# DeltaNet heads of a decoder layer: decay rows asked for earlier and used later, roots a step sooner, the output's finish behind the first terms of the inverse

## The reference

```
qkv = silu(causal_depthwise_conv([b_q, b_k, b_v], conv_w))
q, k = l2_normalize(q), l2_normalize(k)
beta = sigmoid(b_beta);  g = -exp(a_log) * softplus(b_dec + dt_bias)
# per chunk, gcum = cumulated g
decay = exp(gcum_i - gcum_j) on and below the diagonal
A = strict_lower(beta_i * (k k^T) * decay)
u, w = solve(I + A, [v*beta, k*beta*exp(gcum)])
v_new = u - w S;  o = (q*exp(gcum)) S + (tril(q k^T) * decay) v_new
S = exp(g_last) S + (k*exp(g_last - gcum))^T v_new
y_B = rms_norm(o, dn_norm_g) * silu(b_z)
```

## Time and profile before

| what | value |
|---|---|
| median of 3 runs | 1997.52 us (1994.28 to 1998.63) |
| the profiled execution | 1999.72 us, its span 1997.9 us |
| TensorE busy | 1941.1 us, 97% of the span |
| VectorE busy | 940.7 us, 47% |
| ScalarE busy | 760.3 us, 38% |
| GpSimd busy | 81.6 us, 4% |
| mean granted clock of TensorE | 0.99 |
| chain that ended last | TensorE 91% |

### The profile page before, as it was taken

How to read it: one execution, slowest core, us unless ns; L and a number is a source line. 1 busy time by engine, 2 the same in 40 slices (tenths; PEclk the granted TensorE clock), 3 DMA queues, 4 the chain that set the end, 5 groups by cost and what they waited for, 6 DMA issues and landing times.

```text
span 1997.9 us, 25728 instructions
## 1 busy us (share of the span) xinstructions
PE 1941.1 (97%) x9812; PEld 1574.3 (79%) x9812; DVE 940.7 (47%) x1266; ACT 760.3 (38%) x1166; POOL 81.6 (4%) x63
## 2 busy tenths in 40 slices
PE   8999999999989989999999999999999999999996
PEld 6886776777868878888787888788888888888885
DVE  6715565576425353531545663774433223323446
ACT  6335455554342433533343334543223113112331
POOL 0000000001202112020000000000000000000000
PEclk9999999999989999999999999999999999999998
DMA  5232212313121221121534444443321111111144
GB/s 187 99 107 81 78 63 94 126 42 137 64 95 64 85 95 57 71 103 46 211 116 154 141 138 143 163 132 101 95 63 43 52 52 42 52 49 45 51 150 148
DMA packets 62031, 191.51 MB, mean 96 GB/s; under 512 B 6720, under 2 KB 6784, under 8 KB 61952
## 3 DMA queue, kind: packets, MB, share of 16 engines
q1 hardware_dynamic: 58496, 184.13, 27.5%
q10 hardware_dynamic: 3456, 6.29, 0.8%
HBM read 146.33 MB, written 44.07 MB: 95 GB/s over the span
## 4 chain that ended last, share of the span: by engine, by line
PE 91%; DVE 4%; DMA 2%; ACT 2%; issue 2%; ACTq 0%; SPq 0%; DVEq 0%
PE gemm L337 18%; PE gemm L339 17%; PE gemm L338 17%; PE gemm L578 5%; PE gemm L579 5%; PE gemm L580 5%; PE dn L1308 2%; PE dn L1306 2%; PE z L1205 2%; PE gemm L1393 2%; PE dn L1227 2%; PE gemm L1394 2%; PE gemm L1395 2%; PE dn L1304 1%; PE dn L1269 1%
## 5 line engine op out<-in xcount | busy, mean ns | idle before, releaser
L337 PE MATMUL gemm<-act_hi,w_hi 128*128 128x512 f32 x1216 | 508.1, 418 | 0.5 <-issue 0.5
L339 PE MATMUL gemm<-act_hi,w_lo 128*128 128x512 f32 x1216 | 476.9, 392 | 0.0
L338 PE MATMUL gemm<-act_lo,w_hi 128*128 128x512 f32 x1216 | 476.4, 392 | 0.0
L329 DVE TENSOR_TENSOR w_lo<-w_raw,w_hi 128x1024 fp32r<-128x1024 f32 x174 | 215.6, 1239 | 240.6 <-ACT w_hi L324 237.1
L324 ACT ACTIVATE w_hi<-w_raw 128x1024 fp32r<-128x1024 f32 x174 | 183.2, 1053 | 278.2 <-PE gemm L339 153.2
L337 PEld LDWEIGHTS gemm<-act_hi,w_hi 128*128 128x128 f32 x1216 | 230.2, 189 | 56.0 <-issue 18.6
L339 PEld LDWEIGHTS gemm<-act_hi,w_lo 128*128 128x128 f32 x1216 | 229.4, 189 | 49.8
L338 PEld LDWEIGHTS gemm<-act_lo,w_hi 128*128 128x128 f32 x1216 | 230.4, 189 | 41.0 <-issue 3.6
L383 ACT ACTIVATE stage<-gemm,cols 128x512 f32<-128x512 f32 x104 | 71.6, 688 | 239.7 <-PE gemm L339 236.0
L1079 ACT ACTIVATE f_t<-f_t 128x512 f32<-128x512 f32 x64 | 40.4, 632 | 218.0 <-DVE f_t L1909 218.0
L1576 DVE TENSOR_TENSOR_SCAN a_P<-a_keep,a_P,a_floor 128x512 f32<-128x512 f32 (+3 forms) x96 | 93.7, 1006 | 26.1 <-ACT a_keep L869 25.9
(11 more groups left out here) (272 smaller groups left out, 2886.0 us busy)
## 6 DMA issues: line engine op xcount, KB each, us to landing
w_raw<-w_stream SPq DMA_DIRECT2D x174, 512.0 KB, 3.7
projections<-stage SPq DMA_DIRECT2D x60, 512.0 KB, 2.9
gate<-projections SPq DMA_DIRECT2D x48, 256.0 KB, 2.7
d_in<-projections SPq DMA_DIRECT2D x12, 512.0 KB, 5.5
x_sb<-xT SPq DMA_DIRECT2D x8, 512.0 KB, 9.0
x_fin<-xT SPq DMA_DIRECT2D x8, 512.0 KB, 4.4
residual<-mixed ACTq DMA_DIRECT2D x16, 256.0 KB, 2.0
act_hi<-residual SPq DMA_DIRECT2D x8, 512.0 KB, 4.8
```

Source lines behind the costliest of these rows:

```text
L329: nc.vector.tensor_tensor(lo[s][:], raw[s][:].rearrange("p (k c) -> p k c", k=KT), hi[s][:].bitcast(f32), ALU.subtract).then_inc(lo_ready[ ...
L337: nc.tensor.matmul(g_bank[hf][:], w_hi[s][:, k, :], a_hi[:, k, t], start=(k == 0), stop=False)
L338: nc.tensor.matmul(g_bank[hf][:], w_hi[s][:, k, :], a_lo[:, k, t], start=False, stop=False)
L339: last = nc.tensor.matmul(g_bank[hf][:], w_lo[s][:, k, :], a_hi[:, k, t], start=False, stop=(k == KT - 1))
```

## The change

It has four parts. (1) SP asks for the decay rows before the store of block 4, and for the convolution inputs behind that store. (2) VectorE forms the differences at chunk 2 of the scan (was 0) and limits them at chunk 3 (was 1); ScalarE takes roots at chunks 2 and 3 (was 3 and 4), decays at 4 (was 5) and the tail at 5 (was 6). (3) `finish_head(i - 1)` moves from behind gram to behind the vT stage of group 1, once `d_TT` has its first terms. (4) The opening's slots go from 10, 3, 8 to 13, 6, 4.

```diff
-        DN_PRO = [10, 3, 8]
+        DN_PRO = [13, 6, 4]
...
                     if b == 4 and i < 3:
-                        if i < 2:
-                            sp.wait_ge(dn_conv, 12 * i + 24)
-                            load_in(i + 2)
                         for g in range(2):
                             sp.wait_ge(dn_taken[g], 1 + dn_use(i, DN_STAGES.index(f"y{N_LEV - 1}")))
                         load_rows(i + 1)
...
                     if b == 0 and i:
                         store_head(i - 1)
                         load_z(i)
+                    if b == 4 and i < 2:
+                        sp.wait_ge(dn_conv, 12 * i + 24)
+                        load_in(i + 2)
...
                         if n < 3:
                             silu(i + 1, n)
-                        if n in (3, 4):
-                            root_of(i + 1, n - 3)
-                        if n == 5:
-                            decay(i + 1)
-                        if n == 6:
-                            tail(i + 1)
                     if n == 2:
                         exp_ln_tables()
+                    if nxt:
+                        if n in (2, 3):
+                            root_of(i + 1, n - 2)
+                        if n == 4:
+                            decay(i + 1)
+                        if n == 5:
+                            tail(i + 1)
...
-                            if g and i:
-                                finish_head(i - 1)
...
                             nc.vector.scalar_tensor_tensor(d_TT[:, c, :], d_TT[:, c, :], -1.0, mask(ident), ALU.mult, ALU.add).then_inc(dn_tt[g], 1)
+                            if g and i:
+                                finish_head(i - 1)
...
-                        if n == 0:
+                        if n == 2:
                             differences(i + 1)
-                        if n == 1:
+                        if n == 3:
                             limited(i + 1)
```

## The result

The changed kernel takes 2004.24 us (median of 16 runs, 1999.78 to 2006.56) against 1998.55 us (median of 16 runs) for the kernel before: ratio 1.0028, 95% interval 1.002 to 1.0035. It is 5.7 us slower, a small difference but clear of the noise. The profiled execution took 2002.56 us, with a span of 2000.8 us.

The account below looks back on a forecast made before the run. TensorE, busy 97% of the span, was taken as the bound, so only its waits and half-rate stretches count. Terms -24.3 + 1.9 + 6.0 + 10.1 + 9.8 = +3.5 us on 1997.5 gave 2001.0 us, range 1990 to 2007 us.

Parts of the forecast that it names:

- no change: Whole kernel: waits move from the scan to the opening and x1, about the same sum, 1993.5 to 2001.5 us; chance 0.40.
- slower by the clock: TensorE falls to clock 0.50 for 6 us of work at each of four new waits: +7.3 us, 2004.8 us; chance 0.38.
- What bounds the kernel now: TensorE, busy 97% of the span; DeltaNet waits and the half rate after them cost heads 0 and 1 24.3 us together.
- I take the whole 24.3 us as removed: Scan of heads 0 and 1: earlier rows and roots remove all the loss from waits and half rate, 24.3 us.
- The price of +1.9 us: Head 0: a split ahead of the scan's root and another at head's end delay roots and gram, +1.9 us (0 to 3.5).
- Part 4: Opening: the split waits for weights ahead of the roots, so the second squares wait 6.0 us; +6.0 us (3.0 to 6.6).
- qk needs it: Opening: qk needs the end of scale_q, now 499.2 us, or 501.1 us with squares at half rate; loss 4.7 or 6.6 us.
- Part 3: x1 waits 7.7 us in head 1 for weights, 2.9 and 3.5 us later for the store; +10.1 and +9.8 us with clock.
- The clock: Half rate of TensorE after the new waits: 5.8 us for the three waits at x1 together.
- Three out of three waits of 2 us and more: Kernel before: each such TensorE wait was followed by half rate, taken as evidence that the clock falls at new waits.
- The sum: Whole kernel: -24.3 + 1.9 + 6.0 + 10.1 + 9.8 = +3.5 us on the median of 1997.5 us, giving 2001.0 us.
- faster, since the finish is hidden: x1: store and weight load land in time, so the late finish costs nothing; -16.4 us, 1981.1 us; chance 0.22.

Follow-up runs that it names:

- rows and roots: Kernel before with only the earlier rows, later differences and earlier roots, finish and opening as before: 1975.13 us, ratio 0.9887.
- the finish alone: Kernel before with only finish_head moved behind the vT terms of group 1: 2020.14 us, ratio 1.0109.
- the execution of 2005.49 us: The changed kernel unaltered, profiled a third time: 2005.49 us.

## Why the prediction was right or wrong

The forecast of 2001.0 us lay 3.2 us under the median, inside the range. Its likeliest case, no change, was missed by a little: +0.28% is just over the 0.2% that I had set. By the time, the case "slower by the clock", with 2004.8 us and 0.38, is the one that came, within 0.6 us. Its mechanism is not: it had the clock fall at all four new waits and stay down for 6 us of work each time, 9.0 us lost behind x1 and 1.9 us in the opening. In two of the three profiles the clock stayed at 1.00 behind the waits of heads 2 and 3, and the loss was 5.0, 5.5 and 8.0 us in all. That its time is right is luck: the opening cost more than that case had for it.

- **What bounds the kernel now** was right. Taking away the waits gives back more than their length: parts 1 and 2 removed 16.1 us of waits, all 6.3 us lost to the clock, and 22.8 us of time.
- **Parts 1 and 2.** "I take the whole 24.3 us as removed" was right. Alone they gave 22.8 us, and 1.1 us more is the wait for qk's bank, which only part 3 removes. The price of +1.9 us was booked on the wrong part and too low. Its two waits came, 0.87 us at the root in the scan and 0.84 us at gram of head 1, both behind a split. But with parts 1 and 2 alone neither is there; they come with the opening's sum of 23 slots and go with 21. That sum cost 3.7 us on top of rows and roots (1978.8 against 1975.13 us, though one opening wait was saved).
- **Part 4.** The wait of 6.0 us came as 5.91 us, at 488.1 us instead of 487.8 us, and the squares ran at half rate. The term was mis-sized all the same, 6.0 us against 6.8 us (the changed kernel less the one with 10, 3, 10; alone the opening cost 6.2 us). The step that was off is "qk needs it", of `scale_q`: qk also waits until VectorE has read gram's bank, which stands behind `scale_q`. The profile has it as 1.27 us for `d_at`, and qk starts at 501.89 us, not 501.1 us. The larger miss is the one of the line above: with parts 1 and 2 the whole opening cost 10.6 us where the sum had 6.0 + 1.9 us.
- **Part 3.** The mechanism was right in each piece: 8.11 us for 7.7, 2.90 for 3.5, 2.62 for 2.9. The load landed 6.0 us after its issue, where I had assumed 5.3 us. The fixed cost and the rate that the Trainium skill's page "DMA: Bandwidth & Descriptors" gives in the section "Anatomy of one DMA — SWDGE (gpsimd) path" make an estimate of 3.2 us; that fit is for a DMA issued by GpSimd, and this load, issued by SP behind the store and `load_z`, took nearly twice as long. The whole term, 19.9 us, was measured at 18.5 us, or 19.6 us like for like, since the 1.1 us for qk's bank that it gives back stood in the 24.3 us.
- **The clock** was the open size. I gave it 5.8 us for the three waits of x1 and, in the upper figure, 1.9 us for the squares of the opening. The three profiles of the changed kernel have 5.0, 5.5 and 8.0 us for all of it together, and the finish alone 5.6 us more than the kernel before. My size is that of the slower executions, and most of the 16 runs are of that kind by their time and their mean clock. "Three out of three waits of 2 us and more" does not hold as a rule either: with the finish alone the same wait of 2.0 us in the scan was followed by a clock of 1.00.
- **The sum** was 2.2 us too small against the 16 runs. The experiments give it part by part, each on top of the one before: rows and roots -22.8 us, the opening +10.6 us, the finish +18.5 us, together +6.3 us (+5.7 us in the 16 runs; the 0.6 us are the distance between two medians of the kernel before). With the 1.1 us for qk's bank put on the first part as in the prediction, these are -23.9, +10.6 and +19.6 us against -24.3, +7.9 and +19.9 us. So the opening, by the later boundaries above all, is the term that was mis-sized.
- **The rival "faster, since the finish is hidden"** failed as its own counter-argument said, at the explicit wait and at SP's order.

## What to carry to other kernels

An operation that has slack on its own engine may have none at the end of its chain. The finish could be late for VectorE, but a store, a weight load queued behind the store and a reuse of memory hung on it; follow an operation to the last semaphore that it feeds before moving it. In a program where slots hand out shared work, a number in one slot moves every later boundary: changing an opening from 10, 3, 8 to 13, 6, 4 put a split that needs a transfer ahead of a root, moved two later boundaries to worse places, and cost 10.6 us on top of parts 1 and 2 instead of saving the 3.1 us that it aimed at. And a change of several parts is worth taking apart: here parts 1 and 2 are worth -22.8 us, and that version, at 1975.13 us, beats both kernels. Parts measured alone need not add up as they did here by luck; adding them one on top of the other shows what each costs in company.

## What the runs showed of the hardware

TensorE's clock after a wait of 2.0 to 2.9 us is not settled by the wait's length. After 2.90, 2.88, 2.67, 2.66 and 2.62 us it stayed at 1.00; after 2.54, 2.70, 2.78 and 2.83 us it fell to 0.50, in part in the same kernel. A wait of 2.03 us for the same root was followed by 0.50 in the kernel before and by 1.00 with the finish alone. The windows of the execution of 2005.49 us show two stretches at half rate, after its waits of 2.83 and 2.70 us:

```profile
754.00:759.00 5.00, 5.00 (x26) 0.66 0.29 113
867.00:871.00 4.00, 3.20 (x17) 0.57 0.61 211
```

After the three waits of 3.20, 3.25 and 3.33 us, and after all of 5.4 us and more, it fell every time. So a wait of about 3 us has two prices, 3 us or 4.1 to 6.4 us, and the same kernel shows both from one execution to the next. What decides between them no run here shows.

The second operation of the finish took 2.18 us in its old place in heads 1 to 3, with GpSimd at work at the same time, and 1.23 us in its new place, where GpSimd was idle.
